# Two transformer blocks on one core: probabilities divided on ScalarE, paired rotations, a third projection unit prepared early, and a regrouped search in mixer 2

## The reference

```python
# first block: mixer 1
u, f, q, k, v = split(h @ w_in)                      # widths 384, 256, 384, 128, 128
y_ssm = s5_mixer(u, ...)                             # linear state recurrence, both directions, then GLU
y_fft = fourier_mixer(f, w_fft)                      # real part of a 2-D FFT per head
# windowed attention, 6 query heads, 2 key heads, blocks of 128 queries against 3 x 128 keys
m = maximum(max(scores), sink); p = exp(scores - m)
p = p / (sum(p) + exp(sink - m)); y_att = p @ v
x = x + gate * rms_norm(concat(y_ssm, y_fft, y_att) @ w_out); ... convolution FFN
# second block: FFN, layernorm, mixer 2, layernorm, FFN, layernorm
q, c, qi, ki, wi, z = split(x @ w_in_2)
score = sum_h wi_h * relu(qi_h . ki); sel = top_k(score, 256)      # per query
p = softmax(q_abs . c[sel]); att = (p @ c[sel]) @ w_uv
u, v = split(gelu(z)); v = layernorm(v); gm = u * (tril(ws) @ v + bs)
m = concat(att, gm) @ w_out_2
```

## Time and profile before

| | |
|---|---|
| time, median of 3 runs | 3048.61 us (3046.19 to 3049.38) |
| the profiled execution | 3044.93 us, span 3043.1 us |
| busy, share of the span | PE 95%, PEld 75%, DVE 71%, ACT 43%, POOL 8% |
| chain that ended last | PE 78%, DVE 15%, ACT 3%, issue 2%, DMA 1% |
| mean granted clock of TensorE | 0.979 |

### The profile page before, as it was taken

One profiled execution on the slowest core, in us unless ns is written; L12 is line 12 of the kernel. 1 busy time (PEld: TensorE's weight loads), 2 busy tenths in 40 slices (PEclk: granted clock), 3 DMA queues, 4 the chain that ended last, 5 costly groups with the idle time before them and its releaser, 6 DMA issues.

```text
span 3043.1 us, 36909 instructions
## 1 busy us (share of the span) xinstructions
PE 2893.6 (95%) x13273; PEld 2284.8 (75%) x13273; DVE 2159.5 (71%) x3957; ACT 1303.6 (43%) x2282; POOL 228.2 (8%) x251
## 2 busy tenths in 40 slices
PE   6998897999999999999999998998999899999997
PEld 4885676788888888788888875784558678888886
DVE  7888738988888577666665675997525866665668
ACT  3123445544444554333334442576543433333443
POOL 2141200000000000000000001114410000000000
PEclk9988999999999999999999999999999999999999
DMA  6532033244447772444449642110013344445864
GB/s 226 166 125 37 9 132 118 83 159 159 159 159 242 255 240 94 145 159 159 159 156 316 218 144 68 35 39 29 1 41 128 112 155 159 159 159 184 306 201 145
DMA packets 345412, 436.81 MB, mean 144 GB/s; under 512 B 29685, under 2 KB 191517, under 8 KB 345054
## 3 DMA queue, kind: packets, MB, share of 16 engines
q1 hardware_dynamic: 342274, 428.46, 43.2%
q10 hardware_dynamic: 2956, 5.99, 0.5%
HBM read 317.59 MB, written 116.50 MB: 143 GB/s over the span
## 4 chain that ended last, share of the span: by engine, by line
PE 78%; DVE 15%; ACT 3%; issue 2%; DMA 1%; POOL 0%; SPq 0%; DVEq 0%; ACTq 0%
PE psum L1987 36%; PE psum L1438 21%; PE psum L1078 4%; DVE count_junk L3319 3%; PE psum L1978 3%; PE psum L4111 3%; PE psum L3009 2%; PE psum L2988 1%; PE psum L2819 1%; PE psum L2999 1%; PE psum L384 1%; DMA ada_w<-in_w_ada 1%; PE psum L4019 1%; DVE x_t L1684 1%; PE psum L4092 1%
## 5 line engine op out<-in xcount | busy, mean ns | idle before, releaser
L1438 PE MATMUL psum<-far_op,far_op 128*128 128x512 f32 x2772 | 629.6, 389 | 0.0
L1438 PEld LDWEIGHTS psum<-far_op,far_op 128*128 128x128 f32 x2772 | 520.1, 188 | 108.3 <-issue 0.4
L1987 PE MATMUL psum<-x_b,w_near 128*128 128x512 f32 x1440 | 346.1, 389 | 0.8 <-DVE w_near L1610 0.8
L1987 PE MATMUL psum<-x_t,w_near 128*128 128x512 f32 x1440 | 337.1, 389 | 2.3 <-ACT psum L1724 2.3
L1987 PE MATMUL psum<-x_t,w_far 128*128 128x512 f32 x1440 | 336.3, 389 | 0.0
L1987 PEld LDWEIGHTS psum<-x_t,w_near 128*128 128x128 f32 x1440 | 270.1, 188 | 59.6 <-ACT psum L1724 3.5
L1987 PEld LDWEIGHTS psum<-x_b,w_near 128*128 128x128 f32 x1440 | 270.2, 188 | 57.3 <-issue 1.2
L1987 PEld LDWEIGHTS psum<-x_t,w_far 128*128 128x128 f32 x1440 | 270.2, 188 | 56.4 <-ACT u_keep L1736 0.3
L1209 DVE TENSOR_TENSOR far_op<-far_a,far_op 128x512 fp32r<-128x512 f32 x231 | 160.7, 696 | 175.8 <-ACT far_op L1202 174.2
L1202 ACT CAST far_op<-far_a 128x512 fp32r<-128x512 f32 x231 | 143.9, 623 | 316.1 <-PE psum L1438 307.9
L1987 PE MATMUL psum<-x_b,w_far 128*128 128x512 f32 x720 | 176.5, 395 | 9.2 <-DVE val_row L1856 9.2
(11 more groups left out here) (521 smaller groups left out, 4989.2 us busy)
## 6 DMA issues: line engine op xcount, KB each, us to landing
far_a<-row_ops SPq DMA_DIRECT2D x231, 256.0 KB, 3.0
row_ops<-hidden SPq DMA_DIRECT2D x99, 512.0 KB, 5.3
raw<-in_ffn_w SPq DMA_DIRECT2D x88, 512.0 KB, 4.4
col_sums<-hidden SPq DMA_DIRECT2D x66, 512.0 KB, 5.7
far_b<-col_sums SPq DMA_DIRECT2D x132, 256.0 KB, 3.3
raw<-in_w_up SPq DMA_DIRECT2D x44, 512.0 KB, 3.9
...
```

Source lines behind the costliest of these rows:

```text
L1438: ins = t.matmul(bank(b + n), l[slot][:, rows], r[slot][:], start=(fresh and i == 0 and m == 0), stop=(i == FH - 1 and m == 2), skip_group ...
L1987: ins = t.matmul(bank(b), at[:, l, cols], x[:, k, r], start=(start and k == 0 and m == 0), stop=(k == 3 and m == 2), skip_group_check=not ...
```

## The change

In mixer 1, (a) TensorE waits for ScalarE's Fourier copies before it goes on, and for VectorE's two sums at items 4 and 10; (b) the 48 divisions move from GpSimd to ScalarE, one step ahead of the copy of turned probabilities, and the finished block's copy comes ahead of both; (c) VectorE's eight rotation products of a chunk become four over two planes, 128x2x384 each. In mixer 2, (d) the third unit of the in-projection has tiles of its own, and is loaded and split before the second half of the input is complete; (e) `mlp_v` is scaled on VectorE ahead of the loop, and of the last group's bit steps two are ahead of the loop and five at items 5, 14, 17, 20 and 23, with the search closed at item 29.

```diff
-        pe.wait_ge(yf_ready, 3)
+        pe.wait_ge(yf_odd_ready, 3)
...
         for i in range(ITEMS + DELAY + 1):
+            if i == EARLY:
+                pe.wait_ge(yf_ready, 1)
+            elif i == DELAY:
+                pe.wait_ge(yf_ready, 2)
             if EARLY <= i < ITEMS and i % 2 == 0:
...
+        def divide(i):
+            if i % Q_HEADS == 0:
+                act.wait_ge(sums_ready, i // Q_HEADS + 1)
+            p = probs[i % SLOTS][:, 0:P * len(item(i)[4])]
+            s.mul(p, p, att_sum[:, i:i + 1]).then_inc(probs_ready, 1)
...
-            if DELAY <= i < ITEMS + DELAY:
-                copy_probs(i - DELAY)
             if i >= DELAY + 2 and (i - DELAY - 2) % Q_HEADS == Q_HEADS - 1:
                 n = (i - DELAY - 2) // Q_HEADS
                 act.wait_ge(att_mm, Q_HEADS * (n + 1))
                 s.copy(yc_t[:, 5:8, P * n:P * (n + 1)], bank(4, 3 * P).rearrange("p (c q) -> p c q", c=3)).then_inc(att_ready, 1)
+            if DELAY <= i + 1 < ITEMS + DELAY:
+                divide(i + 1 - DELAY)
+            if DELAY <= i < ITEMS + DELAY:
+                copy_probs(i - DELAY)
...
             if part == 0:
-                steps.add(v.tensor_tensor(rot[0][:], sr, tr, ALU.mult))
-                steps.add(v.tensor_tensor(rot[1][:], si, ti, ALU.mult))
-                steps.add(v.tensor_tensor(rot[2][:], si, tr, ALU.mult))
-                steps.add(v.tensor_tensor(rot[3][:], sr, ti, ALU.mult))
+                steps.add(v.tensor_tensor(rot_pair[0], both, both_r, ALU.mult))
+                steps.add(v.tensor_tensor(rot_pair[1], both, both_i, ALU.mult))
...
             elif part == 3:
-                steps.add(v.tensor_tensor(rot[0][:], rot[1][:], tr, ALU.mult))
-                steps.add(v.tensor_tensor(rot[2][:], rot[1][:], ti, ALU.mult))
-                steps.add(v.tensor_tensor(rot[4][:], rot[3][:], ti, ALU.mult))
+                steps.add(v.tensor_tensor(rot_pair[0], rot_pair[1], both_r, ALU.mult))
                 steps.settle()
             elif part == 4:
-                steps.add(v.tensor_tensor(rot[1][:], rot[3][:], tr, ALU.mult))
-                if d:
-                    steps.settle()
+                steps.add(v.tensor_tensor(rot_pair[1], rot_pair[1], both_i, ALU.mult))
+                steps.settle()
...
     def mix_gpsimd(pool, steps):
-        for i in range(ITEMS):
-            if i % Q_HEADS == 0:
-                pool.wait_ge(sums_ready, i // Q_HEADS + 1)
-            p = probs[i % SLOTS][:, 0:P * len(item(i)[4])]
-            nc.gpsimd.tensor_scalar(p, p, att_sum[:, i:i + 1], 1.0, ALU.mult, ALU.mult).then_inc(probs_ready, 1)
         blocks_gpsimd(pool, steps)
...
             nc.scalar.copy(x_hi[:, k, HALF * half:HALF * (half + 1)], column_bank(half, k)).then_inc(cols_hi, 1)
+            if half and k == 4:
+                a_split(act, THIRD)
...
         far_sync(sp, down_1, lambda: mix2_first(sp), nothing)
+        mix2_second(sp)
         for half in range(2):
             end_store(sp, 2, half)
         mix2_sync(sp)
...
-    UNWATCHED, OPEN_AT = (24, 29), (9, 11)
+    UNWATCHED, OPEN_AT, END_SIGNS = (24, 26), (5, 14, 17, 20, 23), 29
...
+    THIRD = 2
+    third_parts = [place(f"third_part{i}", [P, SEQ], RR + 28 * KB + 4 * KB * i, F32R) for i in range(2)]
+
+    def a_parts(n):
+        return third_parts if n == THIRD else (split_hi[n % 2], split_lo[n % 2])
...
+    def mix2_second(sp):
+        for n in range(2, 4):
+            sp.wait_ge(a_lo, n - 1)
+            a_load(sp, n)
...
-        for n in range(2, A_UNITS):
+        sp.wait_ge(keys_ready, 1)
+        sp.dma_start(ki_t[HEAD:P, :], ki_t[0:HEAD, :]).then_inc(keys_in, 16)
+        for n in range(4, A_UNITS):
             sp.wait_ge(a_lo, n - 1)
             a_load(sp, n)
-            if n == A_KEYS + 1:
-
-                sp.wait_ge(keys_ready, 1)
-                sp.dma_start(ki_t[HEAD:P, :], ki_t[0:HEAD, :]).then_inc(keys_in, 16)
...
-        if n >= 2:
+        if n == THIRD:
+            act.wait_ge(f_mm, down_1.mm(FT - 1))
+        elif n >= 2:
             act.wait_ge(a_mm, n - 1)
...
-            if i < NT:
-                scale_values(i)
...
             one(v.tensor_tensor(stat_c[:, 0:NT], v_mean_neg[:], stat_b[:, NT:2 * NT], ALU.mult))
             steps.settle()
-            dve.sem_inc(mv_scaled, 1)
+            for n in range(NT):
+                v.tensor_scalar(mlp_v[:, n, :], mlp_v[:, n, :], stat_b[:, NT + n:NT + n + 1], stat_c[:, n:n + 1],
+                                ALU.mult, ALU.add).then_inc(mv_ready, 1)
...
             if i in OPEN_AT:
                 steps.settle()
                 next_bit(2, UNWATCHED[1] + OPEN_AT.index(i))
-            elif i == OPEN_AT[-1] + 2:
+            elif i == END_SIGNS:
                 end_signs()
```

More of the change, by code:

```diff
@@ L203, in body @@
     turn = [place("turn", [P, 2, PAIRS, NCH], RR + 16 * KB)[:], carry[1][:, :, :, 0:NCH]]
-    rot = [place(f"rot{i}", [P, 3, NCH], XR + (44 + 16 * (i // 2)) * KB + 256 + 1536 * (i % 2)) for i in range(4)]
-    rot.append(place("rot4", [P, 3, NCH], GR + 17 * KB + 512))
+    rot_all = place("rot_all", [P, 2, 4 * KB], XR + 44 * KB + 256)
+    rot_pair = [rot_all[:, :, 3 * NCH * i:3 * NCH * (i + 1)].rearrange("p x (q j) -> p x q j", q=3) for i in range(2)]
+    rot = [rot_pair[i % 2][:, i // 2] for i in range(4)]
     y_rows = place("y_rows", [P, CH, GROUPS * GC], GR + 64 * KB)
@@ L483, in mix_scalar @@
             s.copy(yf_odd[:, pair, :], bank(2 + 2 * pair)).then_inc(yf_odd_ready, 1)
-        s.copy(yc_t[:, 3:5, HALF:HALF + 1], bank(6, 4).rearrange("p (a c) -> p a c", a=2)[:, :, 0:1]).then_inc(yf_ready, 1)
+        s.copy(yc_t[:, 3:5, HALF:HALF + 1], bank(6, 4).rearrange("p (a c) -> p a c", a=2)[:, :, 0:1]).then_inc(yf_odd_ready, 1)
         def exponentials(n, part):
@@ L602, in scan @@
                     steps.add(v.tensor_tensor_scan(dst, decay, src, 0.0, ALU.mult, ALU.add))
+            both_r, both_i = (x.unsqueeze(1).to_broadcast([P, 2, 3, NCH]) for x in (tr, ti))
             if part == 0:
[L605 removed]
+                both = psum[:, 5 * HALF:7 * HALF].rearrange("p (x c) -> p x c", x=2)[:, :, 0:3 * NCH].rearrange("p x (q j) -> p x q j", q=3)
                 dve.wait_ge(states_mm, c + 1)
[L607 to L610 removed]
+                steps.add(v.tensor_tensor(rot_pair[0], both, both_r, ALU.mult))
+                steps.add(v.tensor_tensor(rot_pair[1], both, both_i, ALU.mult))
                 steps.settle()
@@ L2816, in a_step @@
         t, m, slot = nc.tensor, a_width(n), n % 2
-        for i, (l, r) in enumerate(((split_hi, x_hi), (split_hi, x_lo), (split_lo, x_hi))):
+        w_top, w_rest = a_parts(n)
+        for i, (l, r) in enumerate(((w_top, x_hi), (w_top, x_lo), (w_rest, x_hi))):
             for half in halves:
-                ins = t.matmul(bank(2 * slot + half)[0:m], l[slot][:, P * k:P * k + m], r[:, k, HALF * half:HALF * (half + 1)],
+                ins = t.matmul(bank(2 * slot + half)[0:m], l[:, P * k:P * k + m], r[:, k, HALF * half:HALF * (half + 1)],
                                start=(k == 0 and i == 0), stop=(k == KD - 1 and i == 2))
@@ L3106, in mix2_scalar @@
         for n in range(SIGNED):
-            if n >= 2:
+            if n > THIRD:
                 a_split(act, n)
```

21 lines of the change are left out of this document (8 added, 13 removed).

## The result

| | before | after |
|---|---|---|
| median | 3048.99 us (3046.19 to 3052.79, 4 runs) | 3027.62 us (3023.31 to 3029.05, 4 runs) |
| profiled execution | 3044.93 us, span 3043.1 | 3023.31 us, span 3021.5 |
| busy | PE 95%, DVE 71%, ACT 43%, POOL 8% | PE 96%, DVE 71%, ACT 44%, POOL 6% |
| chain | PE 78%, DVE 15%, ACT 3% | PE 82%, DVE 10%, ACT 3% |

The ratio is 0.9927 (0.991 to 0.9944). A second comparison, with five runs of the changed kernel, gave 3022.70 us against 3045.91 and 0.9926 (0.9914 to 0.9939). The forecast was 3026.9, between the two medians of the changed kernel, 0.7 us from the first and 4.2 from the second.

A forecast was written before the change was run, and what follows sets the result against it. TensorE sets the end almost everywhere, VectorE bounds mixer 1. Mixer 1 -8.5, third unit -4.9, ahead of the loop -5.0, loop -3.3: -21.7 from 3044.93 gives 3023.2, median 3.7 above, 3026.9 us; range 3018 to 3038.

The forecast's parts named there:

- the loop: Mixer 2's query blocks: -2.2, -3.3, +1.8 and +0.4 in blocks 0 to 3, sum -3.3 us, bounds -8 and +1.
- the start and the tail: Mixer 1: -2.3 us at the first maximum behind the Fourier sums, +0.9 for the last six divisions.
- The floor of 12.2 for VectorE: Mixer 1: VectorE's need per block after the change, 12.2 us where a block took 13.56.
- The ring at 12.4: Mixer 1: ScalarE and TensorE's cycle sets a block at 12.4 us, 1.15 less; 6.2 blocks give -7.1.
- The fourth rival: Mixer 1: place in the chunk, not GpSimd, slows products and scans; 4.6 us less gain, 3031.5; chance 0.11.
- The ring at 14.0: First rival, mixer 1: ScalarE and TensorE's cycle bounds a block at 14.0 us; 3036.7 in all; chance 0.15.
- the serial one at 19.2: Second rival, mixer 1: turning, division, copy, values run one after another, 19.2 us a block; 3069; chance 0.04.
- A division's pitch: Mixer 1: time from a ScalarE division to the next operation, taken as 0.5 us, bounds 0.4 and 0.7.
- The third unit: Mixer 2's start: -3.4 us of TensorE's wait and -1.5 from a faster matmul pace, -4.9 together.
- Ahead of the loop: Mixer 2: three bit steps leave, eight scalings come, so the loop starts 5.0 us earlier; bounds -3 and -5.3.
- the scalings: Ahead of mixer 2's loop: eight on VectorE at a pitch of about 0.34 us, +2.75 us.

The follow-up runs named there:

- one_wait: The changed kernel with TensorE waiting for both of VectorE's Fourier sums at once, ahead of its next scores; 3028.21 us, one run.
- gp_divide: The changed kernel with the 48 divisions back on GpSimd, paired rotations and order of the copies kept; 3035.26 us, one run.
- block_copy_last: The changed kernel with the finished block's copy behind the division and the copy of turned probabilities again; 3027.49 us, one run.
- single_products: The changed kernel with each wide rotation product written as two of 128x384 again, divisions still on ScalarE; 3027.76 us, one run.
- twice_scaled: The changed kernel with one more ScalarE copy of 128x384 ahead of each division; 3034.40 us, one run.
- third_late: The changed kernel with the third unit's high part cast behind the first unit's result again, early load kept; 3030.64 us, one run.
- values_scalar: The changed kernel with the gated values scaled on ScalarE again, in the first eight items of mixer 2's loop; 3028.84 us, one run.
- bits_spread: The changed kernel with open bit steps at items 5, 14, 22, 30, 37 and the closing at 39; median 3020.20 us, 0.9912 of the kernel before.

## Why the prediction was right

The time came out by the prediction's own steps, with one exception, the loop. That it is within 0.7 us is in part luck: the second comparison is 4.2 off, the first stretch gave -3.7 that nothing ties to the change, the two other unchanged ones +3.0, and the terms that were off partly cancel.

**Mixer 1, the start and the tail.** -2.2 and +1.0 against -2.3 and +0.9. `one_wait` shows that the split wait is the cause of the first; 1.4 to 2.4 of it are left at the end of mixer 1. The tail's +1.0 was met by a sum of two that the prediction didn't make: by `gp_divide` the last divisions cost 1.6 there, and by `block_copy_last` the new order of the copies gives 0.6 back.

**Mixer 1, a block.** The floor of 12.2 for VectorE was right (12.10). The ring at 12.4 was set 0.3 too high, so that the gain is 8.0 and not 7.1 (7.7 to 8.7 by the other traces with this mixer 1). `gp_divide` and `single_products` divide it: 1.2 a block for the divisions' move, through the scans and the products beside GpSimd, and 0.27 for pairing. The fourth rival is refuted: same place, slow only beside GpSimd. The Trainium skill's rule on two-input operations, SBUF — State Buffer, section "Who interferes with whom", fits in kind: the two-input scans and products are slowed and the maximum, with one input from PSUM, is not. How the time is lost the single rows behind `gp_divide` show: a VectorE instruction waits out the division under way, and a division that begins beside a wide product waits too. Beside six divisions, 4.52 together, VectorE paid 0.60 on the scans and 0.64 on both products, which is the 1.23 of the block.

**The rivals in mixer 1.** The ring at 14.0 and the serial one at 19.2 didn't come. `twice_scaled` shows that the first was near: another 0.41 a step makes the ring the bound, at 13.1. A division's pitch of 0.51 lies within the bounds 0.4 and 0.7, at the value taken. The estimate of 0.507 from the Trainium skill, VectorE: DVE Perf Modes, section "The TRN2 errata — SBUF-src ops pay a fixed extra latency per instruction", agrees with that pitch; the row's own length is 0.60. `block_copy_last` shows that the 1.04 of the earlier trace rows would have cost 0.4 to 0.65 a block had it stayed; the prediction counted it as gone, which it is.

**The third unit.** -4.7 against -4.9: 3.3 for the wait and 1.4 for the pace, which follows the granted clock behind the wait (0.52 and 1.00); `third_late` gives both back (3.27 and 1.45).

**Ahead of the loop.** -5.3 against -5.0. One term was mis-sized, the scalings: 3.66 for eight, where 2.75 was worked out from one row of a simpler form. It didn't show, as VectorE was ready 0.33 ahead of TensorE; the shorter hold-up by GpSimd (1.70 in place of 2.31) made up for most of it.

**The loop.** This is the step that failed in its parts: -1.9 against -3.3. Blocks 0 to 4 came out as -2.5, -4.2, +4.5, 0 and +0.3, against -2.2, -3.3, +1.8 and +0.4 for blocks 0 to 3. Block 0's gain was put down to ScalarE alone, though the kernel before ran it at a clock of 0.63, behind TensorE's wait of 5.61 for the bit steps. `values_scalar` is in line with that (5.2 more with block 1, part of it the clock), but the 8.0 is a block at full clock: in three of eight traces it is 11.07, more than before. Block 1 was undersized because TensorE's 15.15 was taken from a block at a clock of 0.91; at 1.00 it works 13.20 there. Block 2 was undersized twice: three steps next to the choosing cost 2.9 to 3.5 (21.8 for 18.9, or for the 18.3 of `bits_spread`), up to 1.1 of it an operation held up by GpSimd, and the lower clock behind their waits 1.6 more in most traces. Why the clock falls in block 2 in seven traces and not in the eighth, and in block 0 in three, isn't settled; no kernel here controls it.

The errors in blocks 0, 1 and 2 partly cancel, and the sum would have been 3 us worse in an execution with a slow block 0, within what runs of one kernel differ by.
